# A norm applied after the projection, its waits moved, and finer hand-offs in the last differential-attention unit

## The reference

```python
hx = modulate(rms_norm_2(x, norm_g[i]), shift_x[:, None], scale_x[:, None])
hc = modulate(rms_norm_2(ctx, norm_g[i]), shift_c, scale_c)
qx, kx, vx, gx = split(hx @ w_in)        # 8 heads of 2 x 64 and 128
qc, kc, vc, gc = split(hc @ w_in)
...                                      # axial rotation of qx, kx
s = jnp.einsum('bqhmd,bkhmd->bhmqk', qb, keys) * ATTN_SCALE
p = jax.nn.softmax(s, axis=-1)
a = p[:, :, 0] - lam * p[:, :, 1]
o = jnp.einsum('bhqk,bkhe->bqhe', a, vals)
o = rms_norm_2(o, subln_g, SUBLN_EPS) * (1.0 - lam_init) * silu(g)
x = x + gate_x[:, None] * (ox @ w_o[i])  # the same for ctx
```

## Time and profile before

| | us |
|---|---|
| median of 3 runs (lowest, highest) | 1640.92 (1640.31, 1641.14) |
| the profiled execution, its own time | 1641.54 |
| its span | 1639.8 |
| TensorE busy | 1555.7 (95%) |
| VectorE busy | 994.5 (61%) |
| ScalarE busy | 757.3 (46%) |
| GpSimd busy | 503.7 (31%) |

### The profile page before, as it was taken

One profiled execution on the slowest core, in us unless ns is written; L12 is line 12 of the kernel. 1 busy time (PEld: TensorE's weight loads), 2 busy tenths in 40 slices (PEclk: granted clock), 3 DMA queues, 4 the chain that ended last, 5 costly groups with the idle time before them and its releaser, 6 DMA issues.

```text
span 1639.8 us, 23714 instructions
## 1 busy us (share of the span) xinstructions
PE 1555.7 (95%) x8392; PEld 1221.6 (75%) x8392; DVE 994.5 (61%) x2286; ACT 757.3 (46%) x1426; POOL 503.7 (31%) x231
## 2 busy tenths in 40 slices
PE   7998999999899999999969999999999989999998
PEld 5886666678688888888857877777777768876566
DVE  6235555355689767646666666675676267147854
ACT  6225766634342413233434544365445343248753
POOL 3651232244244444444211111121214343330012
PEclk9999999999899999999989999999999989999998
DMA  6861112264256565642211111111111112220001
GB/s 198 174 161 33 59 61 75 89 239 139 93 194 196 188 201 185 202 130 91 64 39 39 36 43 39 38 38 38 38 38 52 52 54 90 78 65 14 1 14 64
DMA packets 48401, 149.34 MB, mean 91 GB/s; under 512 B 5782, under 2 KB 9110, under 8 KB 48184
## 3 DMA queue, kind: packets, MB, share of 16 engines
q1 hardware_dynamic: 37080, 112.45, 22.8%
q10 hardware_dynamic: 11232, 35.72, 6.7%
HBM read 141.53 MB, written 6.62 MB: 90 GB/s over the span
## 4 chain that ended last, share of the span: by engine, by line
PE 80%; DVE 7%; ACT 6%; issue 5%; POOL 1%; DMA 0%; ACTq 0%; POOLq 0%; DVEq 0%
PE ps L357 41%; PE ps L361 20%; PE ps L582 4%; PE ps L593 3%; PE ps L563 3%; PE ps L1330 3%; PE ps L1370 3%; PE ps L1342 1%; PE ps L1089 1%; ACT sb L648 1%; ACT w_h L340 1%; PE ps L425 1%; DVE tg L1963 1%; DVE x2l L2036 1%; POOL w_l L985 1%
## 5 line engine op out<-in xcount | busy, mean ns | idle before, releaser
L985 POOL TENSOR_TENSOR w_l<-raw,w_h 128x1024 fp32r<-128x1024 f32 (+1 forms) x190 | 456.2, 2402 | 908.2 <-ACT w_h L340 888.6
L340 ACT ACTIVATE w_h<-raw 128x1024 fp32r<-128x1024 f32 x190 | 200.5, 1057 | 351.0 <-PE ps L357 292.8
L357 PE MATMUL ps<-x2h,w_h 128*128 128x512 f32 (+2 forms) x784 | 233.7, 363 | 34.0 <-DVE ones_r L2317 15.7
L357 PE MATMUL ps<-x1h,w_h 128*128 128x512 f32 x584 | 237.4, 407 | 16.6 <-POOL w_l L985 10.9
L357 PE MATMUL ps<-x1h,w_l 128*128 128x512 f32 x584 | 230.2, 394 | 0.0
L361 PE MATMUL ps<-x1l,w_h 128*128 128x512 f32 x584 | 229.6, 393 | 0.0
L361 PE MATMUL ps<-x2l,w_h 128*128 128x512 f32 (+2 forms) x784 | 220.8, 346 | 0.0
L357 PE MATMUL ps<-x2h,w_l 128*128 128x512 f32 (+2 forms) x784 | 220.3, 345 | 0.0
L357 PEld LDWEIGHTS ps<-x2h,w_h 128*128 128x128 f32 x784 | 126.4, 190 | 63.1 <-issue 19.0
L357 PEld LDWEIGHTS ps<-x1h,w_h 128*128 128x128 f32 x584 | 111.3, 191 | 40.9 <-POOL w_l L985 11.3
L357 PEld LDWEIGHTS ps<-x2h,w_l 128*128 128x128 f32 x784 | 126.6, 189 | 19.5
(11 more groups left out here) (344 smaller groups left out, 2694.7 us busy)
## 6 DMA issues: line engine op xcount, KB each, us to landing
raw<-in_w_mlp SPq DMA_DIRECT2D x64, 512.0 KB, 3.8
mraw<-in_w_mod ACTq DMA_DIRECT2D x51, 512.0 KB, 4.1
raw<-in_w_a SPq DMA_DIRECT2D x32, 512.0 KB, 3.6
raw<-in_w_att SPq DMA_DIRECT2D x25, 512.0 KB, 11.4
raw<-in_w_b SPq DMA_DIRECT2D x20, 512.0 KB, 3.6
raw<-in_w_g SPq DMA_DIRECT2D x16, 512.0 KB, 3.7
raw<-in_w_ao SPq DMA_DIRECT2D x9, 512.0 KB, 3.5
gates<-g_stage ACTq DMA_DIRECT2D x16, 256.0 KB, 2.2
```

The source lines that it names most:

```text
L340: nc.scalar.activation(split(u)[0], raw[:, u % RAW], ACT.Copy).then_inc(w_hi, 1)
L357: mm = nc.tensor.matmul(o, w[:, k], xh(k), start=(first and k == k0 and wi == 0), stop=(last and k == k1 - 1 and wi == 1))
L985: nc.gpsimd.tensor_tensor(l[:, ks], raw[:, u % RAW, ks], h[:, ks].bitcast(F32), ALU.subtract).then_inc(w_lo, 1)
```

## The change

1. **Deferred norm.** TensorE waits for the reciprocal right behind the tile sums and spreads it twice, into banks 7 and 6, ahead of the whole of U_A+2; VectorE starts with two x tiles on bank 7, and multiplies q and k (`evict_pair`) behind the second; ScalarE copies from bank 6, makes two high tiles first and takes q and k then. TensorE waits for the copy before it writes bank 6 again.
2. **The wait for `ones`** stands behind the first eight dense steps of unit 0 and the wait for the gate. Unit 0 begins with 8 steps instead of 9; one more stands in qt = 3, ahead of `turns`.
3. **`take(..., 3)` and `gate_up`** stand at the beginning of the unit that they belong to, no longer at the end of the one before; in the last unit VectorE does tile 0's halves first.
4. **Last unit, ScalarE:** `high(1..3)`, `output_rstd`, `high(4..5)`, the split of U_AO+1, in this order; before, the split, `high(1..5)`, `output_rstd`. VectorE: `output` ahead of `mins(1)`.
5. **Banks freed one by one:** a semaphore of its own behind each half of `take_out`; TensorE's first k step does the tokens' part behind the first and the context's behind the second.

```diff
-        nm3b = Norm(add=0, mm=0)
+        nm3b = Norm(add=0, mm=0, r=2)
...
@@ TensorE, entry
-            first_x(2, 4, 0, 4)
             nm3b.wait(pe, "rc", 1)
             spread(7, 0, 4).then_inc(nm3b.r, 1)
-            first_x(2, 4, 4, KT)
+            spread(6, 0, 4).then_inc(nm3b.r, 1)
+            first_x(2, 4, 0, KT)
             nm3b.wait(pe, "src", KT)
             first_ctx(2, 5, 0, KT).then_inc(unit, 1)
+            pe.wait_ge(n3_r, 1)
             first_ctx(3, 6, 0, KT)
@@ TensorE, partial_out
                         if j:
+                            pe.wait_ge(ao_ev0, j)
+                            products(U_AO + j, out_parts(0)[:1], 0, 1, last=False)
                             pe.wait_ge(ao_ev, j)
-                        else:
-                            pe.wait_ge(ha["g"], KT)
+                            products(U_AO + j, out_parts(0)[1:], 0, 1, last=False)
+                            continue
+                        pe.wait_ge(ha["g"], KT)
@@ TensorE, attend
                 if lead:
-                    dense(9)
+                    dense(8)
                     wait_head(pe, "g", head, 1, 1)
+                    pe.wait_ge(ha["ones"], 1)
...
-                    dense(1 if lead else 2 if more else 4 + (qt == 0))
+                    dense(1 + (qt > 2) if lead else 2 if more else 4 + (qt == 0))
                     turns(qt)
-                    dense(1 + qt // 2 if lead else 1 + qt % 2 if more else 3)
+                    dense(1 + (qt > 1) if lead else 1 + qt % 2 if more else 3)
...
-            pe.wait_ge(ha["ones"], 1)
             all_heads(pe, attend)
@@ ScalarE, entry
-            nm3b.wait(act, "r", 1)
-            nc.scalar.activation(rstd[:, 0:S], ps[:, 7], ACT.Copy).then_inc(n3_r, 1)
+            nm3b.wait(act, "r", 2)
+            nc.scalar.activation(rstd[:, 0:S], ps[:, 6], ACT.Copy).then_inc(n3_r, 1)
...
-            take_first(0, a_q, -0.125).then_inc(ha["q"], 1)
-            take_first(1, a_k, 1.0).then_inc(ha["k"], 1)
             for k in range(KT):
                 nm3b.wait(act, "t", k + 1)
                 shift_tile(k, 0, xn2, 0).then_inc(nm3b.hi, 1)
+                if k == 1:
+                    take_first(0, a_q, -0.125).then_inc(ha["q"], 1)
+                    take_first(1, a_k, 1.0).then_inc(ha["k"], 1)
@@ ScalarE, take_out
-                for w, a, b in ((0, 0, S), (1, S, SC)):
-                    ins = nc.scalar.activation(ao_t[:, j % 2, a:b], pair(0)[:, a:b], ACT.Copy, scale=gcol[:, w:w + 1])
-                ins.then_inc(ao_ev, 1)
+                for w, a, b, done_ev in ((0, 0, S, ao_ev0), (1, S, SC, ao_ev)):
+                    nc.scalar.activation(ao_t[:, j % 2, a:b], pair(0)[:, a:b], ACT.Copy, scale=gcol[:, w:w + 1]).then_inc(done_ev, 1)
@@ ScalarE, attend
+                if c:
+                    take(head, 3, more)
                 if not more:
-                    for k in range(1, KT - 2):
+                    for k in range(1, 4):
                         high(k)
...
                 if c:
                     output_rstd((i, c - 1))
+                if not more:
+                    for k in range(4, KT - 2):
+                        high(k)
+                    split_high(act, U_AO + 1)
...
-                if more:
-                    take((i, c + 1), 3, True)
-                else:
+                if not more:
                     take_out(6)
@@ VectorE, entry
+                    if k == 1 and begun:
+                        begun()
...
+            def evict_pair():
+                v.wait_ge(n3_r, 1)
+                evict_first(0, 0, 1, -0.125)
+                evict_first(1, 2, 3, 1.0)
             invert(v, nm3b, S)
-            v.wait_ge(n3_r, 1)
-            evict_first(0, 0, 1, -0.125)
-            evict_first(1, 2, 3, 1.0)
-            modulated(nm3b, 0, xn2, (0,))
+            modulated(nm3b, 0, xn2, (0,), evict_pair)
@@ VectorE, attend
                 if not more:
                     high_low(0)
+                if c:
+                    gate_up(head)
+                if not more:
                     low(1)
                     low(2)
                 mins(0)
                 if not more:
                     for k in range(3, KT - 2):
                         low(k)
+                if not more:
+                    output((i, c - 1))
                 mins(1)
                 if not more:
-                    output((i, c - 1))
                     low(KT - 2)
...
                 gated(head)
-                if more:
-                    gate_up((i, c + 1))
```

More of the change, by code:

```diff
@@ L521, in build @@
         ao_ev = sem("ao_ev")
+        ao_ev0 = sem("ao_ev0")
         ao_add = sem("ao_add")
@@ L1013, in _ @@
             for j in range(N_OUT):
+                g.wait_ge(ao_ev0, j + 1)
                 g.wait_ge(ao_ev, j + 1)
@@ L2160, in _, with modulated @@
                     g_add(1)
-            def modulated(nm, l, buf, ws):
+            def modulated(nm, l, buf, ws, begun=None):
                 def low(k):
```

## The result

| | before | after |
|---|---|---|
| median of the runs, us (lowest, highest) | 1641.03 (1640.31, 1641.91) | 1624.98 (1624.65, 1625.78) |
| span of the profiled execution, us | 1639.8 | 1622.8 |
| mean granted clock, share of 2.4 GHz | 0.981 | 0.986 |

The ratio is 0.9907, with a 95% interval from 0.9892 to 0.9921: 13.0 to 17.7 us less. The medians differ by 16.05 us, where 14.6 was forecast; the time itself, 1624.98, was forecast as 1626.3, in a range from 1622 to 1631.

The account below looks back on a forecast made before the run. TensorE, busy 95% of the span, was taken as the bound, so only its waits and half-clock time pay. First stretch 11.7 plus last unit 2.9 made 14.6 us; forecast 1626.3 us, range 1622 to 1631.

Parts of the forecast that it names:

- rival A: Unit 0's entry: VectorE's multiply of k does not meet GpSimd, 2.2 us less, 1624.1 us; chance 0.18.
- first meeting in the norm: Deferred norm: VectorE's first `x2l` runs beside GpSimd's low half of U_A+3 and loses 1.6 us.
- `a_k` wait and half clock behind it: Unit 0: the 2.32 us wait shrinks by 1.65 and the half clock behind it goes, -1.3.
- first `ao_t` wait: Last unit: TensorE starts U_AO+1 when ScalarE has evicted the first half, at 1238.8 instead of 1240.41, 1.55 us gained.
- three more: Last unit: three further waits for `ao_t` evictions shrink by 0.45 us each, 1.35 us in all.
- last one, with what follows it: Last unit: the fifth `ao_t` wait gives nothing, as TensorE then waits 0.67 us for the last low tile.
- Meetings with GpSimd: VectorE slowed beside GpSimd: rotated k 0 to 2.4 us, 2.2 taken; first `x2l` 0 to 2.1; `output` taken as 0.
- The clock behind the gap: Unit 0: TensorE's clock falls in the gap ahead of `scores(0)`; its return costs 0 to 1.5 us, 1.5 taken.
- rival B: Last unit: `output` is caught by GpSimd, `mins(1)` comes late, `scores(2)` moves by 1.9 us; 1628.2 us; chance 0.18.
- Rival C: Unit 0 gives 3 us back: `a_k` wait stays 2.3 us, or both norm tiles meet GpSimd; 1629.3; chance 0.12.
- Rival D: Unit 0: the gap only moves, steps taken ahead are missing as filler, all 11.4 us given back; 1638; chance 0.04.
- Rival E: Units 1 to 6: the loop's branch behind the gate's wait makes the kernel slower, 1645 us; chance 0.02.

Follow-up runs that it names:

- x1_null: The kernel before, unchanged, run again: median 1639.01 us, ratio 0.9999 to the kernel before.
- x3_norm: The kernel before with only the deferred norm (part 1 of the change): median 1639.40 us, ratio 0.9994 to the kernel before.
- x5_late: The changed kernel with ScalarE's split of U_A+6 held behind the wait for `ones`: median 1623.78 us, ratio 0.9899 to the kernel before.
- x11_bothhalves: The changed kernel with part 5 undone, TensorE waiting for both eviction halves before the tokens' part: median 1627.54 us, ratio 0.9928 to the kernel before.
- x7_both: The changed kernel with U_A+6's split behind `ones` and eleven dense steps ahead instead of eight: median 1623.91 us, ratio 0.9895 to the kernel before.
- x2_ones: The kernel before with only the wait for `ones` moved behind eight dense steps (part 2): median 1629.61 us, ratio 0.9933 to the kernel before.
- x4_last: The kernel before with only parts 3 to 5 of the change: median 1636.91 us, ratio 0.9980 to the kernel before.
- x6_dense11: The changed kernel with eleven dense steps ahead of the first scores instead of eight: median 1625.66 us, ratio 0.9909 to the kernel before.

## Why the prediction was right, by its steps

The place, the mechanism and the sum held: 14.6 forecast, 13.96 in the changed code, 16.05 between the medians. The time alone wouldn't show it: 1624.98 lies nearer to rival A's 1624.1 than to the 1626.3 of the forecast, and it is the multiply of 2.66 us in the trace that rules A out. The 2.1 us between 13.96 and 16.05 aren't explained by any step; the interval of the ratio, 13.0 to 17.7, holds 13.96, and unchanged code differs by as much between two executions of one program (x1_null).

| step | forecast | measured |
|---|---|---|
| first x tile, clock of before | 818.8 | 818.79 |
| first meeting in the norm | 1.6 | 1.64 |
| later split of U_A+4 | 0.5 | 0.68 (a second `x2l` of 2.38 with 0.41 idle, against 2.11) |
| norm, net | 1.2 | 1.12 (x3_norm) |
| dense steps end, clock of before | 844.9 | 844.66 |
| multiply by `sin_t` caught, lost | 2.2 | 1.97 |
| wait ahead of `scores(0)`, its start | 7.1, 852.0 | 7.37, 852.03 |
| one step more behind it | +1.05 | +1.04 |
| return of the clock, between `scores(0)` and `scores(1)` | +1.5 | +2.35 |
| `a_k` wait and half clock behind it, between `scores(4)` and `scores(5)` | -2.95 | -3.23 |
| first stretch | 11.7 | 11.28 |
| units 1 to 6 | 0 | 0.03 |
| first `ao_t` wait | 1.55 | 1.13 |
| three more | 1.35 | 1.07 |
| last one, with what follows it | 0 | 0.48 |
| last unit | 2.9 | 2.68 |

**Meetings with GpSimd.** This was the step with the widest bounds, and the one that made rival A. x5_late decides it: the same instruction takes 2.66 us beside a low half and 0.69 without one. That it was caught at all was partly luck. The forecast had both starts at 846.7 and gave no reason for the order; on the clock of before GpSimd's was at 846.59 and VectorE's at 846.82, and an instruction that starts first keeps its time (last section). The Trainium skill (GPSIMD Engine Reference, Key points) says that instructions of VectorE with two SBUF inputs contend with GpSimd. The trace agrees: in before, the x tile below, which reads PSUM beside SBUF, began 0.36 us behind the low half at 830.17 and kept its 0.75 us, while the `x2l` at 831.20 became 2.11.

```profile
830.53 0.75 DVE L2030 SCALAR_TENSOR_TENSOR xn<-hc,small,ps 128x512 f32<-128x512 f32 x1
```

**The clock behind the gap** was mis-sized. The forecast took half of the 3.2 us that it read in the earlier trace rows. The return came 5.5 us after TensorE resumed, and 3.0 to 6.4 us after it in the eleven executions in which the clock fell there, and what it costs lay between `scores(0)` and `scores(1)`: 3.27 us apart before (863.40 to 866.67), 5.62 after. The term with the other half clock erred the other way, -3.23 instead of -2.95, and x1_null shows that either can come out 1.4 to 1.5 us otherwise in the same program. That the first stretch was met within 0.4 us is thus in part luck.

**The first `ao_t` wait.** The start of `scores(2)` was forecast at 1235.75 and is 1235.81 on the clock of before. Behind it 0.4 us were lost: U_AO ended at 1238.41, not 1238.1, and the eviction of the first half held TensorE for 0.87 us from there, not 0.7, so that U_AO+1 began at 1239.28 instead of 1238.8 to 1238.9. The three that follow are 0.36 each, not 0.45: of the waits of 0.68, 0.68 and 1.02 us 0.31, 0.31 and 0.65 are left, where the forecast looked for about 0.2 in each. **The last one** was put at nothing, since `last_out` waits for its low tile, and so it does, 1.03 us instead of 0.67. `last_out` came 2.32 us sooner, only 0.12 more than the others had given. The other 0.36 lie behind it: a wait for GpSimd's sums shrank from 1.79 to 1.38. GpSimd had its last `ao_t` sooner; in x11_bothhalves, where it hadn't, that wait is 1.79 again.

**`output` ahead of `mins(1)`** (rival B) met GpSimd as the rival said, but was there first. Timelines of VectorE and of GpSimd after:

```profile
1218.61 1.01 DVE L2254 SCALAR_TENSOR_TENSOR o<-a_g,small,rstd 128x768 f32<-128x768 f32 x1
```

```profile
1218.77 3.08 POOL L986 TENSOR_TENSOR w_l<-raw,w_h 128x1024 fp32r<-128x1024 f32 x1 [20.23 <-DVE x2l L2260]
```

The one that started 0.16 us sooner kept its time, and the low half took 3.08 us instead of 2.40, with nobody waiting for it. The second minimum of `mins(1)` ended at 1235.74 on the clock of before, forecast at 1235.7.

**Rival C** did not come: the `a_k` wait fell to 0.43, and the norm's tiles lost 1.64 and 0.68. **Rival D** did not for the eight steps, and did for three more (x7_both). **Rival E**: units 1 to 6 kept their length within 0.03 us, so that the branch costs nothing there.

## What to carry to other kernels

When a wait is moved behind work that doesn't need it, price what that work sets free on the other engines, too: here 4.1 of the 7.4 us that TensorE still waited came from two low halves that GpSimd started in the middle of VectorE's chain, and holding both back was worth 4.5 us of the first stretch, 4.1 of them in that wait. Filler that is taken ahead pays only as far as nothing else was waiting for its old place; look for the next wait in the same unit, and whether it is work or only the order of an engine's list that makes it. A difference between two traces should be divided by anchors in unchanged code before any of it is credited to an edit, and even a stretch that agrees can hide two differences of the clock that cancel.

## What the runs showed of the hardware

- Who starts first keeps its time when VectorE and GpSimd meet. GpSimd first: VectorE's instruction ends 0.55 to 0.56 us behind it, whenever it began (0.75 became 2.39, 0.69 became 2.66 and 2.86). VectorE first, by 0.16 us: it took its 1.01 us, GpSimd 3.08 instead of 2.40. In units 1 to 6 of before the multiply by `sin_t` of k starts 0.31 us ahead of a low half each time (947.99 and 948.30 in unit 1) and keeps 0.69 us, and the low half takes 2.58 to 2.59.
- Two wide SBUF inputs aren't the only case. In the last unit of before `a_p<-a_p,small` (line 2280), which reads one wide tile and a scalar for each partition, takes 0.62 us at 1238.09 and 2.73 at 1242.25, beside the low half that began at 1242.14.
- A stall of TensorE alone doesn't decide whether its clock falls. Behind the 1.25 us wait for the first `ao_t` it fell in x2_ones and x3_norm, at 1.5 us each, and not in before or x1_null, with the same instructions. Behind the 2.32 us wait for `a_k` it fell in before, x3_norm, x4_last, x6_dense11 and x7_both, and not in x1_null.
- One program took 2.65 us more in one execution than in another ahead of its 790th microsecond (before and x1_null), where its clock was at 0.50 for 20.5 and 13.7 us.
